# A reordered opening, and attention endings split by groups of heads, in a four-layer fp32 model kernel

## The reference, cut to what matters

```
for each of 8 steps m:                       # c is one vector, two of them in all
    shift, scale, gate = split(silu(c) @ w_mod[m] + b_mod[m], 3)
    h = rms_norm(x, g[m]) * (1 + scale) + shift
    x = x + gate * fn_m(h)
# fn: 0 short convolution (w_in 1024x3072, three taps, w_out), 1 SwiGLU 2816,
#     2 dilated attention (15 heads), 3 mixture of 8 experts, top 2,
#     then rms_norm(x, final_g), and twice: 4/6 attention, 5/7 SwiGLU 2816
```

```
y = concat(rms_norm(ya, ga), rms_norm(yb, gb), rms_norm(yc, gc))
x = x + gate * (y @ w_o)
```

## Time and profile before

| | |
|---|---|
| time, median of 3 runs | 2013.88 us (2011.97 to 2018.26) |
| the profiled execution | 2016.78 us, of which the span from first to last instruction is 2014.6 |
| TensorE products, busy | 1877.4 us, 93% of the span |
| VectorE, busy | 1635.9 us, 81% |
| ScalarE, busy | 1137.4 us, 56% |
| granted TensorE clock, mean | 0.986 |
| moved from HBM | 548.38 MB |

### The profile page before, as it was taken

One profiled execution on the slowest core, in us unless ns is written; L12 is line 12 of the kernel. 1 busy time (PEld: TensorE's weight loads), 2 busy tenths in 40 slices (PEclk: granted clock), 3 DMA queues, 4 the chain that ended last, 5 costly groups with the idle time before them and its releaser, 6 DMA issues.

```text
span 2014.6 us, 29326 instructions
## 1 busy us (share of the span) xinstructions
PE 1877.4 (93%) x9242; PEld 1553.8 (77%) x9242; DVE 1635.9 (81%) x2173; ACT 1137.4 (56%) x1616; POOL 36.1 (2%) x47
## 2 busy tenths in 40 slices
PE   1899999988999999999999999978799999779998
PEld 1887888877788888888888888866678887667886
DVE  6988886768999999998989989898786659776554
ACT  1434444453777777777777777655544444544442
POOL 2000000000000000000000000000000000000000
PEclk9999999999999999999999999989899999899999
DMA  8877997557699999999999999958468875845762
GB/s 284 318 280 254 357 362 227 155 169 235 221 369 331 370 336 369 334 355 345 346 355 343 358 339 363 333 197 236 155 213 270 272 240 160 259 141 181 217 219 73
DMA packets 368506, 551.08 MB, mean 274 GB/s; under 512 B 35859, under 2 KB 293142, under 8 KB 368374
## 3 DMA queue, kind: packets, MB, share of 16 engines
q1 hardware_dynamic: 365424, 547.81, 81.6%
q10 hardware_dynamic: 2118, 1.46, 0.3%
q0 software_dynamic: 832, 0.30, 0.1%
HBM read 548.38 MB, written 1.08 MB: 273 GB/s over the span
## 4 chain that ended last, share of the span: by engine, by line
PE 80%; DVE 12%; ACT 4%; issue 2%; DMA 1%; POOL 0%; DVEq 0%; ACTq 0%; POOLq 0%
PE ps L402 24%; PE ps L404 24%; PE ps L403 24%; DVE units_low L397 2%; PE ps L952 2%; PE ps L898 2%; ACT prob L1266 2%; PE ps L1072 1%; DVE mod_acc L1574 1%; DVE x_tokens L1601 1%; DVE x_normed L1600 1%; DMA mod_in<-in_mod_w 1%; PE ps L885 1%; PE ps L915 1%; PE ps L715 1%
## 5 line engine op out<-in xcount | busy, mean ns | idle before, releaser
L397 DVE TENSOR_TENSOR units_low<-raw_units,units_high 128x1024 fp32r<-128x1024 f32 (+2 forms) x840 | 982.1, 1217 | 102.8 <-ACT units_high L393 97.6
L393 ACT ACTIVATE units_high<-raw_units 128x1024 fp32r<-128x1024 f32 (+2 forms) x840 | 844.9, 1058 | 240.1 <-PE ps L404 219.2
L402 PE MATMUL ps<-units_high,hT_high 128*128 128x512 f32 (+2 forms) x1576 | 621.4, 394 | 8.9 <-DVE hT_low L1643 4.3
L404 PE MATMUL ps<-units_high,hT_low 128*128 128x512 f32 (+2 forms) x1576 | 618.1, 392 | 0.0
L403 PE MATMUL ps<-units_low,hT_high 128*128 128x512 f32 (+2 forms) x1576 | 613.9, 390 | 0.0
L402 PEld LDWEIGHTS ps<-units_high,hT_high 128*128 128x128 f32 (+1 forms) x1576 | 296.7, 188 | 75.6 <-issue 5.9
L404 PEld LDWEIGHTS ps<-units_high,hT_low 128*128 128x128 f32 (+1 forms) x1576 | 296.4, 188 | 65.5
L403 PEld LDWEIGHTS ps<-units_low,hT_high 128*128 128x128 f32 (+1 forms) x1576 | 296.5, 188 | 64.4 <-issue 0.2
L402 PE MATMUL ps<-units_high,aT_high 128*128 128x512 f32 x632 | 258.8, 410 | 1.2 <-DVE qkT L1811 0.6
L404 PE MATMUL ps<-units_high,aT_low 128*128 128x512 f32 x632 | 248.3, 393 | 0.0
L403 PE MATMUL ps<-units_low,aT_high 128*128 128x512 f32 x632 | 246.4, 390 | 0.0
(11 more groups left out here) (277 smaller groups left out, 1394.0 us busy)
## 6 DMA issues: line engine op xcount, KB each, us to landing
raw_units<-in_moe_w_gate SPq DMA_DIRECT2D x352, 256.0 KB, 4.6
raw_units<-in_moe_w_up SPq DMA_DIRECT2D x352, 256.0 KB, 5.7
raw_units<-in_moe_w_down SPq DMA_DIRECT2D x176, 512.0 KB, 6.3
mod_in<-in_mod_w SPq DMA_DIRECT2D x96, 512.0 KB, 5.8
mod_in<-in_w_mod SPq DMA_DIRECT2D x96, 512.0 KB, 5.3
...
```

Of the source, the lines that this page charges most:

```text
L393: eng.activation(whi[:rows, n % H, 0:width], raw[:rows, n % R, 0:width], ACT.Copy).then_inc(f.hi, 1)
L397: eng.tensor_tensor(low[:rows, n % R, 0:width], raw[:rows, n % R, 0:width], whi[:rows, n % H, 0:width].bitcast(F32), ALU.subtract).then_in ...
L402: pe.matmul(dst, ah, bh, start=start, stop=False, **kw)
L404: return pe.matmul(dst, al, bh, start=False, stop=stop, **kw)
```

## The change

Three places.

*Opening.* SP issues four blocks of w_mod, then x, then three units, then the other twelve blocks. VectorE makes the rope angles before it waits for the columns. ScalarE sums the squares of x (four halves, semaphore `s_sq0`) and makes the high parts of three units before its part of x_normed. VectorE makes the low parts of units 1 to 4 between the chunks of `hT_low`. TensorE runs four fp32 products of 128x512 into an unused bank as soon as 13 blocks are done.

*Router.* The whole second tile is transposed back before the ranks, and the two filler products (`bridge`) in front of them go.

*Endings of the attentions of steps 4 and 6.* ScalarE takes the sinks' exponentials and the squares of group 2 (heads 10 to 15) right after the last exponentials, in front of the last two copies of probT. VectorE scales heads 10 to 15, then 0 to 7, then 8 and 9, in six instructions; roots are taken in two chains, groups 0 and 2, then group 1. The value products of heads 8 and 9 wait for the scaling of heads 10 to 15, which lie in the same bank. The chunks of y go in the pair order 0, 3, 1, 2 (`Y_PAIRS`), w_o's units likewise; the last two pairs are transposed behind the second unit of the projection, and their low parts come behind the low parts of two more units.

```diff
@@ -111,6 +111,7 @@
 SP_LATER = 6
+CONV_UNITS_FIRST = 3
@@ -438,6 +440,9 @@
     GROUPS = ((0, 256), (256, 640), (640, 1024))
+    G_AT = (0, 4, 2)
+    Y_PAIRS = [(0, 1, 2, 3, 4), (0, 3, 1, 2), (0, 3, 1, 2)]
+    Y_CHUNK = lambda a, c: 2 * Y_PAIRS[a][c // 2] + c % 2
@@ -511,8 +516,11 @@
+        mods(MOD_SLOTS)
         sp.dma_start(x[:, :, :], g["x"].rearrange("b (t p) d -> p (b t) d", p=P)).then_inc(s_x, 16)
-        mods(MOD_COLS)
+        for k in range(CONV_UNITS_FIRST):
+            issue_unit(sp, fa, N_CONV_IN, k, 0, blocks(g["conv_w_in"][0], 512)(k))
+        mods(MOD_COLS - MOD_SLOTS)
@@ -530,7 +538,7 @@
         conv_in, conv_out = blocks(g["conv_w_in"][0], 512), rows_of(g["conv_w_out"][0])
-        for k in range(32):
+        for k in range(CONV_UNITS_FIRST, 32):
@@ -570,7 +578,7 @@
                 bias_load(1 + l, nth)
-            phase(fb, n0 + N_WO2, 8, rows_of(g["w_o_2"][l]))
+            phase(fb, n0 + N_WO2, 8, lambda k: rows_of(g["w_o_2"][l])(Y_CHUNK(1 + l, k)))
@@ -762,7 +770,7 @@
-        def project_out(f, n0, chunks, rows, ready, conv=False):
+        def project_out(f, n0, chunks, rows, ready, conv=False, free=None, beside=None):
@@ -775,6 +783,8 @@
+            if free is not None:
+                pe.wait_ge(*free)
@@ -787,6 +797,8 @@
                     sum_gate(0)
+                if beside is not None and k == 1:
+                    beside()
@@ -887,6 +899,8 @@
                     pe.wait_ge(s_pte, i0 + j + 1)
+                    if second and j == n - 2:
+                        pe.wait_ge(s_ho, 6 * (a - 1) + 2)
@@ -900,16 +914,15 @@
-        def y_transposes(a):
+        def y_transposes(a, first, end):
...
             w = KR if a == 0 else P
-            chunks = W1 // KR if a == 0 else DC
-            for pair in range(chunks // 2):
+            for pair in range(first, end):
...
                 for i in range(2):
-                    c = 2 * pair + i
+                    c = Y_CHUNK(a, 2 * pair + i)
@@ -988,6 +1001,9 @@
+        pe.wait_ge(s_mused, MOD_COLS - 3)
+        for _ in range(4):
+            pe.matmul(ps[:, 2, :], ident, table[:, 0:512], start=True, stop=True)
@@ -1051,8 +1067,7 @@
         back(0, 4, 8).then_inc(s_hb, 1)
-        back(1, 0, 4)
-        bridge(2, 2)
+        back(1, 0, 8).then_inc(s_hb, 1)
@@ -1060,7 +1075,6 @@
         pe.matmul(ps[:, 1, 3 * E:4 * E], lower, m1, start=False, stop=True).then_inc(s_rk, 1)
-        back(1, 4, 8).then_inc(s_hb, 1)
@@ -1153,8 +1167,9 @@
             attention(1 + l)
-            y_transposes(1 + l)
-            project_out(fb, n0 + N_WO2, DC, P, lambda k: (s_yTl, 2 * YT0[1 + l] + k + 1))
+            y_transposes(1 + l, 0, 2)
+            project_out(fb, n0 + N_WO2, DC, P, lambda k: (s_yTl, 2 * YT0[1 + l] + k + 1),
+                        free=(s_ho, 6 * (l + 1)), beside=lambda: y_transposes(1 + l, 2, 4))
@@ -1268,6 +1283,8 @@
                     split_high(ac, f, n_out + p, 0, rows)
+                if p == (n - 1) // 2 and ending is not None:
+                    ending()
@@ -1284,16 +1301,15 @@
-        def yT_high(a):
+        def yT_high(a, first, end):
             w = KR if a == 0 else P
-            chunks = W1 // KR if a == 0 else DC
-            for c in range(chunks):
+            for c in range(first, end):
...
                 else:
-                    gcol = V_GG + 8 * (a - 1) + c
+                    gcol = V_GG + 8 * (a - 1) + Y_CHUNK(a, c)
@@ -1304,8 +1320,15 @@
         ac.activation(rope_cs[:, :, :, :], rope_ang[:, :, :, :], ACT.Sin).then_inc(s_rot[1], 1)
+        ac.wait_ge(s_x, 16)
+        for t in range(T):
+            for half in range(2):
+                ac.activation(xn[:, t, half * 512:(half + 1) * 512], x[:, t, half * 512:(half + 1) * 512], ACT.Square,
+                              scale=1.0 / 32, accum_out=small[:, 100 + 2 * half + t:101 + 2 * half + t])\
+                    .then_inc(s_sq0, 1)
+        highs(fa, N_CONV_IN, 0, CONV_UNITS_FIRST)
         xn_half(0)
-        highs(fa, N_CONV_IN, 0, AHEAD)
+        highs(fa, N_CONV_IN, CONV_UNITS_FIRST, AHEAD)
@@ -1478,18 +1501,26 @@
             transposed(3, 7)
-            attention(1 + l, fb, n0 + N_WO2)
-            ac.wait_ge(s_al, 2 + l)
-            ac.activation(ale[:, :, 0:6], ale[:, :, 0:6], ACT.Exp).then_inc(s_ale, 1)
-            for nth, (out_of, t, grp) in enumerate(((1, 0, 0), (2, 1, 0), (3, 0, 1), (3, 0, 2), (4, 1, 1))):
+            def group_square(t, grp, scaled):
                 c0, c1 = GROUPS[grp]
-                ac.wait_ge(s_ho, 4 * l + out_of)
-                ac.activation(qkT[:, 4 + 2 * nth:6 + 2 * nth, :].rearrange("p a b -> p (a b)")[:, 0:c1 - c0],
-                              xn[:, t, c0:c1], ACT.Square, scale=(c1 - c0) ** -0.5, accum_out=ssx[:, 0, 2 * grp + t:2 * grp + t + 1])\
-                    .then_inc(s_gsq, 1)
-            yT_high(1 + l)
-            highs(fb, n0 + N_WO2, AHEAD, 8)
+                ac.wait_ge(s_ho, 6 * l + scaled)
+                ac.activation(qkT[:, 4 * grp + 2 * t:4 * grp + 2 * t + 2, :].rearrange("p a b -> p (a b)")[:, 0:c1 - c0],
+                              xn[:, t, c0:c1], ACT.Square, scale=(c1 - c0) ** -0.5,
+                              accum_out=ssx[:, 0, G_AT[grp] + t:G_AT[grp] + t + 1]).then_inc(s_gsq, 1)
+            def sink_and_last_group():
+                ac.wait_ge(s_al, 2 + l)
+                ac.activation(ale[:, :, 0:6], ale[:, :, 0:6], ACT.Exp).then_inc(s_ale, 1)
+                for t in range(T):
+                    group_square(t, 2, 1 + t)
+            attention(1 + l, fb, n0 + N_WO2, ending=sink_and_last_group)
+            group_square(1, 0, 4)
+            group_square(0, 1, 5)
+            yT_high(1 + l, 0, 4)
+            highs(fb, n0 + N_WO2, AHEAD, AHEAD + 2)
+            yT_high(1 + l, 4, 8)
+            highs(fb, n0 + N_WO2, AHEAD + 2, 8)
@@ -1528,12 +1559,6 @@
         ve.memset(qkT[32:33, 0, 0:6], 1.0)
-        ve.wait_ge(s_vt, 1)
-        ve.tensor_copy(cols[:, :], ps[:, 7, 0:V_ROWS]).then_inc(s_cols, 1)
-        ve.wait_ge(s_rpi, 16)
-        ve.tensor_copy(qkv[0:120, 640:671], qkv[0:120, 600:631][:, ::-1]).then_inc(s_rpr, 1)
@@ -1556,6 +1581,12 @@
+        ve.wait_ge(s_vt, 1)
+        ve.tensor_copy(cols[:, :], ps[:, 7, 0:V_ROWS]).then_inc(s_cols, 1)
+        ve.wait_ge(s_rpi, 16)
+        ve.tensor_copy(qkv[0:120, 640:671], qkv[0:120, 600:631][:, ::-1]).then_inc(s_rpr, 1)
@@ -1601,9 +1632,9 @@
-        def summed_rstd(before, done=None):
-            ve.wait_ge(s_sq, before + PARTS)
+        def summed_rstd(summed, done=None):
+            ve.wait_ge(*summed)
@@ -1622,7 +1653,7 @@
             else:
-                summed_rstd(before, (s_rstd, s + 1))
+                summed_rstd((s_sq0 if s == 0 else s_sq, before + PARTS), (s_rstd, s + 1))
@@ -1778,11 +1808,10 @@
         ve.wait_ge(s_x, 16)
-        norm(0)
+        norm(0, 0)
...
         mod_cols(0)
-        lows(fa, N_CONV_IN, 1, AHEAD)
-        hT_low(0)
+        hT_low(0, after={1 + 2 * k: lambda k=k: lows(fa, N_CONV_IN, 1 + k, 2 + k) for k in range(AHEAD - 1)})
@@ -2144,21 +2173,53 @@
             link(ve.reciprocal(ale[:, :, :], xstat[:, 1, :, :]))
-            heads_out(1 + l, s_ho)
-            ve.wait_ge(s_ho, 4 * (l + 1))
-            c0, c1 = GROUPS[2]
-            link(ve.tensor_tensor_reduce(out=qkT[:, 0:2, :].rearrange("p a b -> p (a b)")[:, 0:c1 - c0],
-                                         in0=xn[:, 1, c0:c1], in1=xn[:, 1, c0:c1], scale=1.0 / (c1 - c0), scalar=0.0,
-                                         op0=ALU.mult, op1=ALU.add, accum_out=ssx[:, 0, 5:6]))
-            ve.wait_ge(s_gsq, 5 * (l + 1))
-            link(ve.tensor_scalar(ssx[:, 0, 0:6], ssx[:, 0, 0:6], EPS, None, ALU.add))
-            rsqrt(ssx[:, 0, 0:6], ssx[:, 1, 0:6], ssx[:, 2, 0:6], ssx[:, 3, 0:6])
-            for i, (c0, c1) in enumerate(GROUPS):
+            def heads_scaled(h0, h1):
+                last = max(HEAD_ORDER.index(h) for h in range(h0, h1))
+                ve.wait_ge(s_pv, HEADS_BEFORE[1 + l] + 1 + last)
                 for t in range(T):
-                    ve.tensor_scalar(xn[:, t, c0:c1], xn[:, t, c0:c1], ssx[:, 1, 2 * i + t:2 * i + t + 1], None,
-                                     ALU.mult).then_inc(s_y, 1)
-            yT_low(1 + l)
+                    at = (h0 % 8) * HD
+                    ve.tensor_tensor(
+                        xn[:, t, h0 * HD:h1 * HD].rearrange("p (h d) -> p h d", d=HD),
+                        ps[:, 2 * t + h0 // 8, at:at + (h1 - h0) * HD].rearrange("p (h d) -> p h d", d=HD),
+                        ale[:, t, h0:h1][:, :, None].broadcast_to((P, h1 - h0, HD)), ALU.mult).then_inc(s_ho, 1)
+            def group_square(t, grp):
+                c0, c1 = GROUPS[grp]
+                return ve.tensor_tensor_reduce(
+                    out=qkT[:, 4 * grp + 2 * t:4 * grp + 2 * t + 2, :].rearrange("p a b -> p (a b)")[:, 0:c1 - c0],
+                    in0=xn[:, t, c0:c1], in1=xn[:, t, c0:c1], scale=1.0 / (c1 - c0), scalar=0.0,
```

(27 more changed lines are left out.)

16 lines of the change are left out of this document (8 added, 8 removed).

## The result

The changed kernel takes 2001.77 us (median of 6 runs, 2000.53 to 2006.21) where the kernel before takes 2014.49 (6 runs): a ratio of 0.9938 [0.9928, 0.9947], 12.5 us of gain where 20.2 were forecast. The profiled execution spans 2000.8 us against 2014.6. Two later series of the same kernel gave 0.9924 [0.9905, 0.9943] and 0.9926 [0.9914, 0.9938]; the mean of the three is 0.9929, or 14.2 us.

The account below looks back on a forecast made before the run. Matrix products hold 80% of the chain, so the winnable time was taken to lie in the seams. Opening 12.0, router 0.7, endings 3.0 and 4.5 sum to 20.2 us, from 2013.88 to 1993.7; range 1988 to 2002.

Parts of the forecast that it names:

- Order of the steps: Opening and endings: first convolution product 7.4 us after E; last layer's residual 29.5 us after the last exponential.
- E: Opening: end of product 15 of `mod_acc`, 42.76 before, put at 38.4, 4.4 us earlier.
- Rope angles (1): Opening: angles moved behind the column copy let the first `mod_acc` product start 3 to 4.7 us earlier.
- The loads (2): Opening: x and three units queued early fill a DMA hole; product 4's load still lands when needed, about 17.2.
- The sign of error: Opening: the forecast is wrong if waits for `mod_in` or `raw_units` grow beyond 3 us before 110.
- Squares, warm-up, low parts (3 to 5): Opening: squares save 2.3 us, column sums fall from 6.63 to 3.7, first convolution product comes at 45.8, not 56.65.
- What becomes late next (6): Convolution: low part 20 ends at 102.4, the gating wait near 102.2 instead of 114.10, a gain of 12.0 us.
- Router (7): Router: earlier transposes and no filler products give VectorE back 0.7 us (0 to 0.9).
- Endings (8): Endings of the later attentions, by head groups: 3.0 us in the last layer, 4.5 in the earlier one.
- The sum: Whole kernel: 12.0 + 0.7 + 3.0 + 4.5 = 20.2 us of gain, median 1993.7.
- A: Opening paced by the loads, giving only 6 to 8 us: 1998 to 2000; chance 0.17.
- B: Endings give nothing, leaving a gain of 12.7 us: 2001; chance 0.11.

Follow-up runs that it names:

- e13: The changed kernel unedited, run again beside two variants on one chip: 2000.32 us, ratio 0.9926 to the kernel before.
- e5: The changed kernel unedited, profiled a second time: 1999.45 us, ratio 0.9924 to the kernel before.
- e11: The changed kernel with the rope angles ahead of the column copy again: 2003.06 us, ratio 0.9939 to the kernel before.
- e12: The kernel before, unedited, profiled once more: 2016.36 us, ratio 1.0001.
- e2: The kernel before with the edits of the two endings alone: 2009.38 us, ratio 0.9974.
- e3: The changed kernel with the first three units' loads behind all sixteen `mod_in` loads: 2002.29 us, ratio 0.9932 to the kernel before.
- e9: The changed kernel with early units behind all `mod_in` loads and ScalarE's high parts between chunks of hT: 1997.11 us, ratio 0.9901 to the kernel before.
- e10: The changed kernel with e9's edits, and late value products ahead of the last prob transposes in both later attentions: 2000.09 us, ratio 0.9918 to the kernel before.
- e14: The same edits to the changed kernel as e9, run again beside e13: 2000.08 us, ratio 0.9926 to the kernel before.
- e15: The same edits to the changed kernel as e10, run again beside e13: 1998.51 us, ratio 0.9911 to the kernel before.
- e4: The changed kernel with the three early units issued behind the load of `mod_acc` product 11: 2002.94 us, ratio 0.9939 to the kernel before.
- e7: The changed kernel without the four warm-up products and their wait: 2003.06 us, ratio 0.9939 to the kernel before.
- e8: The changed kernel with low parts 1 to 4 in front of the chunks of hT again: 2004.36 us, ratio 0.9949 to the kernel before.
- e1: The kernel before with the opening's edits alone: 2006.51 us, ratio 0.9956.

## Why the prediction was right or wrong

**Order of the steps: right.** In the first profile every distance came as forecast: normalisation, sums and first product after E, and the residual after the last exponential in the last layer. The first product came at E + 8.8 in e13, and that residual at 31.5 and 31.7 us in e5 and e13, so part of this agreement is the luck of one profile.

**Rope angles (1): right, but worth little.** The start came at 12.08; e11 shows that its 4.8 us are 2.0 at E.

**The loads (2): wrong, the first failed step.** "Product 4's load is issued at 13.8 and lands at about 17.2" reckoned the bytes ahead of it, 5.3 MB, as "gone by about 15.6 us at the 398 GB/s of a full stretch". The trace of the kernel before has 190 GB/s in its first 7 us and 406 from 7 to 12, so the row was there to be read. The changed kernel moved 202 GB/s in its first 7 us, 406 from 7 to 12 and 338 from 12 to 18: 5.5 MB by 18 us, where I had 5.3 by 15.6, and product 4 began at 20.61. E was 40.16, not 38.4. The sign of error that I had named, `mod_in` waits over 3 us, came true (7.6 us, the longest 3.7). Part of the 42.76 that I started from was also one execution's: e12 and e2 have 40.89 and 42.40. The 1.8 us between 38.4 and 40.16 are what the kernels with the units behind (e3, e9, e10, e14, e15) win back at E in the mean. That the early units held product 4 back is shown by e3, e4, e9 and e14, where it started between 17.1 and 17.6.

**Squares, warm-up, low parts (3 to 5): right in kind.** e7 prices the warm-up at 1.4 us in the mean and 2.1 in the best profiles, because it often ends behind E; in those it brought the sums from 5.90 to 3.84 us, where the forecast had 6.63 and 3.7. e8 prices the interleaving at 3.5, and at 5.0 with the clock that it guards (4 us in the ratio). The squares alone were not tried. The prediction puts the old column sums "mostly at the lower level". The granted clock reads 1.00 through them, in the kernel before as in e7; what the rows show is their pace, 421 ns for a product at the median without the warm-up and 275 with it.

**What becomes late next (6): right path, wrong last wait, and the 12.0 too large.** The forecast let low 20 end the wait, at 102.4. It ran from 100.67 to 101.89 and TensorE's own end, E + 62.8 as forecast, was the last: this is what made up about 1.0 of the 1.8 us that E missed. The first profile's 11.1 flatters the opening, though. The mean of three profiles is 10.2, and e1, with the opening alone, gained 8.9 by its ratio (6.2 to 11.5 by its interval). Neither the DMA nor low 20 held TensorE after 47.48: ScalarE waited 24.1 us for `raw_units` between 40 and 104, and nobody behind it missed anything. The windows of 398 and 402 GB/s of both kernels lie above the about 358 GB/s that the Trainium skill (DMA: Bandwidth & Descriptors, Specifications) gives as a core's limit from HBM. At the 281 ns pace the same opening ends the wait at 105.2, 9.1 us before e12's.

**Router (7): small.** 0.4 us for 0.7, in every kernel that has the edit (0.4 to 0.5) and in none without it. ScalarE's wait of 1.37 us for the second copy is gone: both copies run without a gap from 504.19 to 506.13. In its place ScalarE waits 1.00 us for the gather (L1086) ahead of the second high part.

**Endings (8): the second failed step.** The 4.5 of the earlier layer counted on the clock staying up in the new order. The gap of 1.72 us before the last transposes of `prob` was left in place, the clock fell behind it as before, and the gain was the 3.0 to 3.2 of two endings that both have the fall. I had worked out 3.5 for that case and taken 4.5. In the last layer 2.7 stood for 3.0 in the first profile, where the clock fell in neither kernel. In e5 and e13 it fell in the new ending, against a first profile of before without the fall, and 1.0 and 0.8 were left. The clock fell behind T0 in 17 of 22 changed endings and in 4 of 6 old ones, and the slack of 1.6 us on VectorE that was to cover "most of a slow clock" did not: the residual moved from 29.8 to between 31.5 and 31.7 us. The two endings were put at 7.5 and gave 5.0 by the means.

**The sum** then misses 0.9 + 0.3 + 0.3 + 1.5 = 3.0 us of terms, 17.2 instead of 20.2. The other 3.4 us down to the first profile's 13.8 are the loss of 2.9 in step 4's attention and 0.5 ahead of the router. The loss is the third failed step, a term put at nothing: the forecast took every stretch outside the edits as fixed. It is 0.1 to 3.0 us in the sixteen profiles beside the first of before (2.9, 0.3 and 2.0 in three of the changed kernel, 1.8 in e12).

The loss goes with TensorE's clock. Between 1333 and 1413 us of the kernel before, nine of the 17 profiles lost 0 to 0.3 us, and in each of them the granted clock was 0.50 for 6.0 to 6.6 us of the stretch. The other eight lost 1.1 to 3.0 us, and there it was 0.50 for 9.6 to 14.7 us. The same stretch in the kernel before, in e5 and in e13 (the clock is the third number from the end):

```profile
1332.75:1413.16 80.41, 71.33 (x364) 56.03 (x365) 70.49 (x141) 41.72 (x79) 3.73 (x4) 0.96 0.71 210
```

```profile
1322.60:1403.30 80.70, 71.37 (x364) 56.18 (x365) 70.49 (x141) 41.81 (x79) 3.74 (x4) 0.96 0.71 208
```

```profile
1321.70:1404.10 82.40, 72.32 (x364) 57.65 (x364) 70.58 (x141) 41.55 (x79) 3.74 (x4) 0.92 0.71 204
```

In the first profile of the changed kernel (2.9 us) one `mod_in` load was also 1.8 us later than before. Which comes first, the thinner work or the lower clock, and why one execution has it and the next has not, stays open. The attention of step 6 varies too, by 1.5 us of gain to 2.1 us of loss.

The 2001.77 lies inside the stated range, but by luck. It is the figure of rivals A and B (1998 to 2000, and 2001), and neither came: the opening gave more than A's 6 to 8, and the endings gave 5, not nothing. No single term makes the difference: in the mean of the three profiles the opening, the stretch ahead of step 4's ending and both endings came out 1.4 to 1.9 us short each, and 0.8 us came back between the endings.
